# Weighted values of a sliding-window attention: four products of 256 columns in place of eight of 128, with ScalarE moving the results to head order

## What is computed

```python
def sink_swa_attention(q, k, v, sinks):
    ...
    s = jnp.einsum('bnqhgd,bnkhd->bnhgqk', qb, kb) * ATT_HDIM ** -0.5
    ...
    m = jnp.maximum(jnp.max(s, axis=-1, keepdims=True), sink)
    p = jnp.exp(s - m)
    denom = jnp.sum(p, axis=-1, keepdims=True) + jnp.exp(sink - m)
    o = jnp.einsum('bnhgqk,bnkhd->bnqhgd', p / denom, vb)
    return o.reshape(B, S, ATT_WIDTH).astype(q.dtype)
```

## Time and profile before

| | |
|---|---|
| median of 3 runs | 2254.19 us (2253.38 to 2257.12) |
| the profiled execution | 2256.47 us, its span 2254.8 us |
| TensorE busy | 2199.8 us of the span (98%) |
| ScalarE busy | 750.6 us (33%) |
| VectorE busy | 1214.5 us (54%) |
| granted TensorE clock, mean | 0.997 |

### The profile page before, as it was taken

The page is one execution under the profiler, slowest core; times in us unless marked ns, Lnnn a source line. Parts: engine busy times, 40 slices in busy tenths (PEclk is TensorE's granted clock), DMA queues, the critical chain, the costliest instruction groups (busy, mean ns, idle before and its releaser), DMA issues.

```text
span 2254.8 us, 36218 instructions
## 1 busy us (share of the span) xinstructions
PE 2199.8 (98%) x13083; PEld 1778.6 (79%) x13083; DVE 1214.5 (54%) x2150; ACT 750.6 (33%) x1521; POOL 227.8 (10%) x150
## 2 busy tenths in 40 slices
PE   7998999999999999999999999999999999999998
PEld 4676788888887778888888778888888877888886
DVE  3567683866767564252555845234354665515344
ACT  3554533343355331111235532113024444212012
POOL 2322345444300000000000000000000000000000
PEclk9999999999999999999999999999999999999999
DMA  9965598888663446555464335655546344555554
GB/s 359 400 225 196 198 342 300 289 294 286 224 239 123 169 172 237 187 193 199 177 233 152 137 144 205 228 201 186 195 167 239 133 165 149 204 187 193 199 187 149
DMA packets 114444, 476.99 MB, mean 212 GB/s; under 512 B 7936, under 2 KB 38922, under 8 KB 69258
## 3 DMA queue, kind: packets, MB, share of 16 engines
q1 hardware_dynamic: 114313, 475.24, 57.9%
HBM read 372.45 MB, written 102.76 MB: 211 GB/s over the span
## 4 chain that ended last, share of the span: by engine, by line
PE 86%; DVE 7%; ACT 2%; issue 2%; DMA 2%; SPq 1%; DVEq 0%; POOL 0%; POOLq 0%; ACTq 0%
PE ps L614 18%; PE ps L615 18%; PE ps L616 18%; PE ps L639 8%; PE ps L640 8%; PE ps L641 8%; PE ps L716 1%; PE ps L677 1%; PE ps L567 1%; DMA AWZ<-in_w_ada_dram 1%; PE ps L758 1%; ACT SM L1266 1%; PE ps L688 1%; DVE PT L1673 1%; PE ps L880 1%
## 5 line engine op out<-in xcount | busy, mean ns | idle before, releaser
L614 PE MATMUL ps<-hTh,wt 128*128 128x512 f32 x1920 | 757.9, 395 | 5.8 <-DVE hTl L1589 4.3
L616 PE MATMUL ps<-hTh,wt 128*128 128x512 f32 x1920 | 747.8, 389 | 0.0
L615 PE MATMUL ps<-hTl,wt 128*128 128x512 f32 x1920 | 747.7, 389 | 0.0
L614 PEld LDWEIGHTS ps<-hTh,wt 128*128 128x128 f32 x1920 | 360.4, 188 | 92.6 <-issue 18.7
L616 PEld LDWEIGHTS ps<-hTh,wt 128*128 128x128 f32 x1920 | 360.4, 188 | 76.0
L615 PEld LDWEIGHTS ps<-hTl,wt 128*128 128x128 f32 x1920 | 360.7, 188 | 71.5
L1853 DVE TENSOR_SCALAR cv<-ub,CW 128x512 f32<-128x512 f32 x176 | 98.5, 560 | 466.4 <-ACT ub L1406 451.9
L1406 ACT ACTIVATE ub<-ps 128x512 f32<-128x512 f32 x176 | 105.4, 599 | 685.2 <-PE ps L616 685.2
L639 PE MATMUL ps<-wt,pTh 128*128 128x512 f32 x692 | 270.1, 390 | 0.0
L641 PE MATMUL ps<-wt,pTh 128*128 128x512 f32 x692 | 269.3, 389 | 0.0
L640 PE MATMUL ps<-wt,pTl 128*128 128x512 f32 x692 | 269.2, 389 | 0.0
(11 more groups left out here) (270 smaller groups left out, 2144.7 us busy)
## 6 DMA issues: line engine op xcount, KB each, us to landing
wt<-split_w SPq DMA_DIRECT2D x264, 1024.0 KB, 4.8
split_w<-wt SPq DMA_DIRECT2D x88, 1024.0 KB, 7.0
raw<-in_w_up_dram SPq DMA_DIRECT2D x22, 1024.0 KB, 9.6
XT<-in_w_ada_dram SPq DMA_DIRECT2D x10, 1024.0 KB, 11.6
XN<-in_x_dram SPq DMA_DIRECT2D x4, 2048.0 KB, 11.5
raw<-in_w_in_dram SPq DMA_DIRECT2D x8, 1024.0 KB, 15.0
XR<-in_x_dram SPq DMA_DIRECT2D x4, 2048.0 KB, 9.4
raw<-in_w_down_dram SPq DMA_DIRECT2D x8, 1024.0 KB, 9.3
```

Of the source, the lines that this page charges most:

```text
L614: mm(ps[:, bank, :], w, hTh[:, k, :], start=(k == 0), stop=False)
L615: mm(ps[:, bank, :], w, hTl[:, k, :], start=False, stop=False)
L616: ins = mm(ps[:, bank, :], wl[:, slot, k, :], hTh[:, k, :], start=False, stop=(k == KD - 1))
```

## The change

`weighted_values` now gives the whole TensorE column range 0 to 63 to query half c = 0 and 64 to 127 to c = 1, and takes all four heads (256 columns) in one matmul. So eight instructions of 128 columns become four of 256: two with `VS` and `VA` on all 128 rows, and two with `VD`, each on 64 rows and 64 columns. The two with `VS` and `VA` are issued before the wait for the masked probabilities, the two with `VD` after it. The results of pass x lie in bank 5 + x % 2 and no longer wait for `att_lo` of the pass before, but for the moves of two passes before.

Partitions 0 to 63 of a result now hold query half 0 of all four heads, partitions 64 to 127 hold half 1. `att_high` therefore first moves the result in four ScalarE copies of 64 partitions and 128 columns from PSUM to `T2` in head order (two of them to the other partition half), waits for them, and then rounds from `T2` into `ATT`. `att_low` subtracts from `T2` too. A move also waits for the `att_lo` of two passes before, which read the same half of `T2`.

```diff
@@ TensorE: weighted_values
-                    if x_:
-                        pe.wait_ge(s["att_lo"], b * 8 + x_)
-                    else:
+                    if x_ >= 2:
+                        pe.wait_ge(s["att_moved"], b * 32 + 4 * (x_ - 1))
+                    if x_ == 0:
                         pe.wait_ge(s["vd_ready"], b * 3 + 3)
                     pe.wait_ge(s["p_copied"], b * 8 + x_ + 1)
+                    kv = slice(hh * 64, hh * 64 + 64)
+                    bank = 5 + x_ % 2
+                    for c in range(2):
+                        mm(ps[64 * c:64 * c + 64, bank, 0:256], VA[:, t + 1, kv] if c else VS[:, t, kv],
+                           PT[:, x_ % 2, 1, :, 64 * c:64 * c + 64], start=True, stop=False)
                     fenced(s["p_masked"], b * 16 + 2 * x_ + 2)
-                    kv = slice(hh * 64, hh * 64 + 64)
-                    for c in range(2):
-                        for par in range(2):
-                            mm(ps[64 * par:64 * par + 64, 5 + c, 0:128], VA[:, t + 1, kv] if c else VS[:, t, kv],
-                               PT[:, x_ % 2, 1, 2 * par:2 * par + 2, 64 * c:64 * c + 64], start=True, stop=False)
                     for c in range(2):
                         r = slice(64 * c, 64 * c + 64)
-                        for par in range(2):
-                            ins = mm(ps[64 * par:64 * par + 64, 5 + c, 0:128], VD[r, t, kv],
-                                     PT[r, x_ % 2, 0, 2 * par:2 * par + 2, r], start=False, stop=True)
+                        ins = mm(ps[r, bank, 0:256], VD[r, t, kv], PT[r, x_ % 2, 0, :, r], start=False, stop=True)
                     ins.then_inc(s["pv_mm"], 1)
@@ ScalarE: att_high
                     act.wait_ge(s["pv_mm"], b * 8 + x_ + 1)
-                    act.activation(ATT[:, t, 0, 2 * hh:2 * hh + 2, :].rearrange("p j (c q) -> p j c q", c=2),
-                                   ps[:, 5:7, 0:128].rearrange("p c (j q) -> p j c q", j=2), ACT.Copy)\
+                    if x_ >= 2:
+                        act.wait_ge(s["att_lo"], b * 8 + x_ - 1)
+                    for par in range(2):
+                        for c in range(2):
+                            r, q = slice(64 * c, 64 * c + 64), slice(64 * par, 64 * par + 64)
+                            act.activation(T2[q, x_ % 2, 0:256].rearrange("p (j c q) -> p j c q", j=2, c=2)[:, :, c, :],
+                                           ps[r, 5 + x_ % 2, 128 * par:128 * par + 128].rearrange("p (j q) -> p j q", j=2),
+                                           ACT.Copy).then_inc(s["att_moved"], 1)
+                    act.wait_ge(s["att_moved"], b * 32 + 4 * x_ + 4)
+                    act.activation(ATT[:, t, 0, 2 * hh:2 * hh + 2, :],
+                                   T2[:, x_ % 2, 0:256].rearrange("p (j q) -> p j q", j=2), ACT.Copy)\
                        .then_inc(s["att_hi"], 1)
@@ VectorE: att_low
-                    halves = lambda i: ATT[:, t, i, 2 * hh:2 * hh + 2, :].rearrange("p j (c q) -> p j c q", c=2)
-                    tt(halves(1), ps[:, 5:7, 0:128].rearrange("p c (j q) -> p j c q", j=2),
-                       halves(0).bitcast(fp32), ALU.subtract).then_inc(s["att_lo"], 1)
+                    pair = lambda i: ATT[:, t, i, 2 * hh:2 * hh + 2, :]
+                    tt(pair(1), T2[:, x_ % 2, 0:256].rearrange("p (j q) -> p j q", j=2),
+                       pair(0).bitcast(fp32), ALU.subtract).then_inc(s["att_lo"], 1)
```

More of the change, by code:

```diff
@@ L263, in hymba_block @@
           tok_tr tok_taken dstate_mm state_ready pool_ready pool_mm intra_mm hgo_mm hgo_taken oss_ready or_ready g_softplus g_sub g_exp o_squared o_ready hgt_tr
-          k_copied att_hi att_lo p_norm p_norm_a recip vd_ready p_masked s_mm row_max probs es_ready p_tr p_copied pv_mm tile_done half_ready premul fin_r fin_done conv_done gelu_done
+          k_copied att_moved att_hi att_lo p_norm p_norm_a recip vd_ready p_masked s_mm row_max probs es_ready p_tr p_copied pv_mm tile_done half_ready premul fin_r fin_done conv_done gelu_done
           prod_ready ph_ready p_ready y_added act_steps dve_steps dve_up act_ada pool_steps pe_fence dve_fence
```

## The result

The changed kernel takes 2282.26 us as the median of 4 runs (2280.27 to 2284.05), the kernel before 2255.65 us beside it (2253.38 to 2259.58): a ratio of 1.0116, 95% interval 1.0098 to 1.0134, so 22 to 30 us slower. The profiled execution took 2282.6 us with a span of 2280.9 us, 26.1 us more than the span before. The forecast was 2266.3 us with a range up to 2277: the sign is right, and about half of the loss is missing from it.

A forecast was written before the change was run, and what follows sets the result against it. TensorE, busy 2199.8 of 2254.8 us, was taken as the bound. Loop losses of 3 x 3.4 = 10.2 us plus 1.9 us in the first block made 12.1 us, giving 2266.3 us on the median, range 2258 to 2277 us.

The forecast's parts named there:

- The VS and VA pair, unchanged at 0.59 us: TensorE in weighted_values: columns per half stay the same, so the time to the first VD matmul stays 0.59 us.
- The VD pair, 0.59 us in place of 0.38: TensorE in weighted_values: two diagonal quarters at once, 256 columns each, take 0.59 us, making a product 1.18 us.
- the rule of the Trainium skill weighed in the prediction: L884's pair: row tiles cannot access one PSUM bank simultaneously; if serial, 0.43 us more per product, 13.6 us in all.
- The moves, 0.30 us apart and no overlap: ScalarE in att_high: four copies start 0.30 us apart without overlap, 1.23 us per product; forecast case, chance 0.5.
- The waits: TensorE, second block: about 1 us at L865 in passes 6 and 7, 1.2 before the last L884, none for att_moved.
- The loops, 12.1 us: Attention loops of four blocks: 1.9 us longer in the first, 3.4 us in each other one, 12.1 us in all.
- the walk: Second block's loop, ScalarE pass by pass: ScalarE sets the pace from about pass 4; loop ends at 748.1 against 744.66.
- TensorE's waits elsewhere do not depend on this loop, so nothing gives the delay back: Outside the loops: nothing offsets the 12.1 us, which is added whole to the kernel's time.
- Overlapping moves: Rival, ScalarE's moves: starts 0.17 us apart, 7.6 us slower in all, 2261.8 us; chance 0.2.
- serial quarters: Rival, L884's VD pair: diagonal quarters one after the other, 0.43 us more per product, 26 us, 2280 us; chance 0.12.
- Faster: Rival, TensorE in the loops: early VS and VA pair fills the mask's wait, 5 to 6 us less, 2249 us; chance 0.06.

The follow-up runs named there:

- the experiment without a change of half: Kernel before, its TensorE program untouched, plus four ScalarE copies of 64x128 into T2, none to the other partition half, and the rounding copy: 2272.21 us, ratio 1.0068.
- the three versions that have moves and full instruction count: Kernel before with four moves added, 2272.21 us; changed kernel with eight 128-column product instructions, 2271.36 us; the latter with its moves in another order, 2270.10 us.
- the padded kernel before: Kernel before with 128 semaphore increments added at the start of TensorE's program: 2273.43 us, ratio 1.0065.
- before + 256: Kernel before with 256 semaphore increments added at the start of TensorE's program: 2283.08 us in one run.
- changed + 64: Changed kernel with 64 semaphore increments added at the start of TensorE's program: 2278.94 us in one run.

## Why the prediction was right on the loop and wrong on the sum

**The VS and VA pair, unchanged at 0.59 us.** Right: 0.58 us.

**The VD pair, 0.59 us in place of 0.38.** Right: 0.58 us. Two diagonal quarters write one PSUM bank side by side; one after the other they would have taken 1.0 us. So the rule of the Trainium skill weighed in the prediction (TensorEngine Tiling (Array Packing), Gotcha 1) is not borne out for time here.

**The moves, 0.30 us apart and no overlap.** Right: 0.295 us, and the experiment without a change of half shows that L1240, which changes halves too, was the better row to go by than the full-width copies, though it reads `F` and not PSUM.

**The waits.** Right in place and size: about 0.75 us at L865 in passes 6 and 7 of the second block (1.0 was forecast), 1.07 us ahead of the last VD pair (1.2), no TensorE wait for `att_moved`.

**The loops, 12.1 us.** Measured from each loop's first value product to the first transpose behind the loop (L935, after L933): 1.9 us in the first block (1.9 forecast), and 3.1, 3.1 and 3.3 us in the others (3.4 each): 11.4 us. The rounding copy lasts 0.418 us, not 0.386; the walk made ScalarE's passes a little too long all the same, and which stretch of it is not taken apart.

**"TensorE's waits elsewhere do not depend on this loop, so nothing gives the delay back", and a sum over the loop alone.** This is the step that failed. TensorE's instructions were counted to price them, and never to ask where the code behind them comes to lie. Everything outside the loops stood in the sum at nothing. What that brought, read by matching the large products of the two traces one by one (how far the lag grows at each place):

| term | us |
|---|---|
| three issue stalls (2.2, 3.4, 2.2; 2.05, 3.26, 2.05 of it idle) | 7.8 |
| half clock behind each, 3 x 1.65 | 5.0 |
| the first block's way into the output projection (L639 waits for L1596) | 1.3 |
| half clock at 253.9 us in the first block | 1.5 |
| half clock at 1338 us of the kernel before, not in the changed one | -1.0 |
| the four loops | 11.4 |
| sum | 26.0 |

The spans differ by 26.1. The first two terms are shown by experiment: they go when the instruction count is restored or the code shifted back, stay when the moves are dropped, and come up in the kernel before by padding alone. The first-block wait at L639, two pieces instead of one, follows the moves: the three versions that have moves and full instruction count show pieces of up to 1.7 or 2.0 us there (1.6 before), and the one without moves has 1.6. Stretches at half clock like the one at 253.9 us stand in every kernel at some of the block's waits of up to 2.1 us for `XN` at L677 or just behind them, and which of these waits has one differs from kernel to kernel (the padded kernel before has one at 255.2 us; the plain one has none there, but at 795.7, 1338.4 and 1881.2 us). Why was not tried, so these two terms are read and not explained. The kernel before with the early wait shows the step failing the other way, if by less: 5.6 us gained in its loops, 4.8 in its span.

**The rivals.** Overlapping moves and serial quarters are both excluded by the rows above. The time measured lies near that of the serial quarters, 2280 us, for a wholly different reason: the total alone would have pointed at the wrong mechanism. "Faster" named the right gain, the early VS and VA pair, and 5 to 6 us for it; alone it shortens the loops by 5.6 us, and the time by 0.15% or 3.4 us (1.4 to 5.4).

**What stays open** is why the fetch comes late at just these places when the code is half a packet off. Instruction packets come all the time (one every 4 to 17 us around the loop in the kernel before, every 4 to 22 us in the changed one) and do no harm. Position is not everything either: before + 256 has a stall in the first block that the kernel before, at the same position, has not, and changed + 64 has two there.

The Trainium skill (Runtime: NRT & Kernel Launch, Instruction fetch mechanics) says that instructions are fetched in blocks of 16 KiB, 256 instructions, that crossing a block's boundary is mostly hidden, and that a taken branch to a block which isn't there costs a fetch. The traces agree on the packet's size and on "mostly": 81 packets, three stalls. The stall at 1178 us lies 8 us behind the jump back to the block's start (1170.0 us). The two others lie in straight code, over 90 us behind the last jump; by that page they would not be looked for.

## What to carry to other kernels

Shortening or lengthening an engine's program moves everything behind it against the blocks in which it is fetched; when that engine is the bound, look for stalls without a releaser, and compare against a version with the same instruction count before blaming the change's own work. A TensorE stall of 2 us costs more than itself, since the clock behind it may be halved for a while. And when a change has one part that costs nothing, time that part alone: here a wait moved behind four products beats both kernels, while the whole rearrangement costs 26 us, about half of it in stalls and stretches at half clock outside its own work.

## What the runs showed of the hardware that was not expected

- Fetch stalls of 1.3 to 3.3 us on TensorE, each with one 16384-byte packet that takes 0.9 to 1.1 us, after which TensorE goes on 1.2 to 1.5 us later. Three of them came wherever the code lay 128 or 129 instructions off where it lay before, and at none of the shifts 0, 1, 63, 65 and 256; at 65 and 256 single ones came in the first block.
- Behind most of these stalls the granted clock is 0.5 (1.2 GHz) for 3.41 us: about 1.65 us more for 512-column matmuls. Behind the first stall of the version without moves (2.33 us) and the 1.37 us one with 256 increments it stays at 1.
- ScalarE copies of 64x128 out of PSUM, 0.26 to 0.27 us each, start 0.17 to 0.18 us apart where both read and write the same partition half (from two banks), and 0.28 to 0.30 us apart where either half changes.
- Semaphore increments on TensorE start 0.151 us apart at the start of the program (128 of them, 19.3 us).
